# New values of a gated delta rule from (beta v - beta k state), the output norm's column sums one head later, and the last output tile in two token passes

## The chip, the cores and the metric

The kernel runs on one NeuronCore of a Trainium2 chip. The metric is the device time of the whole program in microseconds (us). Before the change it is 1100.43 us, the median of 3 runs (1100.04 to 1100.97).

## The reference

One decoder layer over 16 learned meta tokens and 512 tokens of width 1024, in float32. Two mixers work side by side (a gated delta rule of 8 heads, and a short gated convolution), are merged by gates and projected; a SwiGLU feed-forward block of width 2816 follows, and a last RMS norm. Cut to what matters here:

```python
# per head, chunks of 64 tokens
a_mat = jnp.where(strict, (k_beta @ k.T) * decay, 0.0)
rhs = jnp.concatenate([v_beta, k_beta * jnp.exp(gc)[..., None]], axis=-1)
sol = lax.linalg.triangular_solve(a_mat + eye, rhs, left_side=True, lower=True)
u_val, w_cum = sol[..., :dv], sol[..., dv:]
def step(state, xs):
    v_new = u_i - w_i @ state
    o_i = q_i @ state + qk_i @ v_new
    state = state * gl_i[..., None, None] + k_i.T @ v_new
    return state, o_i
o = rms_norm(o, o_norm) * jax.nn.silu(z)
...
h = h + mixed @ w_o
gt, up = jnp.split(rms_norm(h, norm2) @ w_gate_up, 2, axis=-1)
return h + (jax.nn.silu(gt) * up) @ w_down      # then the final rms_norm
```

With T = (a_mat + I)^-1 the new values are T (beta v) - (T (beta exp(gc) k)) state. They are also T (beta v - beta exp(gc) k state): the same sum, the solve last.

## The kernel before, in words

Everything lies transposed, features on the partitions and the 512 tokens (528 with the meta tokens) along the row. All weights come as one stream of 162 blocks of 128x1024 (`BLOCKS`, then `DOWN` blocks of the last projection). SyncE loads a block, ScalarE rounds it to its high part (`split_weights`, `w_hi`), GpSimd subtracts to get the low part (`w_lo`), and TensorE multiplies each of the block's 8 tiles three times (high by high, high by low, low by high; `products`, L911). So TensorE's stream is one long row of such products, 24 of 512 columns for a narrow block, 48 of 258 or 264 for a wide one.

The delta rule is woven into that stream. Each engine has a generator `delta_steps` with 28 steps a head; TensorE takes a step after every second tile, four a block, and the other engines take four in the period of a block, with the work on the last block's result (`evacuate`) and the splits of the next block's weights in between. Every engine runs its queue in order, the order is fixed by this code, and semaphores carry the rest. Seven blocks, and so one round of 28 steps, belong to a head: q, k, v, z, c, u, b. The rule's steps 0 to 3 lie in block b, 4 to 7 in the next head's q, and so on to 24 to 27 in its u.

A head's round, as the prediction uses it:

- Step 0, TensorE: K K^T (four 128x128 products, L972), turns of the meta tokens (L976, L977), turns of K (L981). VectorE: `am` (the masked matrix), then two operations on `tm`, three small ones, the short convolution's work on block u, and in step 1 `um`, the transpose of `tm` (L721), which the solve needs. Step 1, TensorE: Q K^T (L988).
- Step 3, TensorE: the solve's first product, `um` by `alev` (L1009); then it alternates to step 14 with ScalarE's copies and VectorE's updates.
- Step 15: W = K_beta T (four products, L1055), which ScalarE turns to `nwt`. Steps 16 to 22: for each of four pieces of 128 tokens the new values (`um` by `vb` and `nwt` by `state` in one bank, L1065 and L1066), ScalarE's copy `vnew`; steps 17 to 23: the state's update and the output.
- Steps 24 to 27: the output's norm. ScalarE squares the output (L505), VectorE adds the term of q (L765), ScalarE rounds (`qo_hi`), VectorE subtracts (`o_lo`), TensorE sums over the features with a matrix of ones (`spread_sums`, step 26), ScalarE takes the inverse root (L531), VectorE scales, ScalarE and GpSimd split the result (`og_hi`, `og_lo`). In the same steps the next head's k is normalised (k_root), its decay factors made (`decay_factors`, `xt`), its v turned (L1098) and scaled (`vb`).

At the end the last of 8 output tiles (L1160) has 66 products of 512 columns; then the tile is added to the residual (L902), squared (L644), summed by TensorE (L1166), the root taken (L646), all 8 tiles scaled (L905) and each sent out (L269).

Of the kernel before, what the change touches and what calls it, by code (L numbers as in the profile page):

```python
# [3 lines left out]
D = 1024  # L4
T = 512
META = 16
L = META + T
HALF = L // 2
TAIL = META - 4
HEADS = 8  # L10
# [15 lines left out]
DOWN = FT * KT // 8  # L26
STREAM = MAIN + DOWN
# [4 lines left out]
STEPS = 28  # L32
PRE = 20
# [28 lines left out]
def hybrid_block_kernel(nc, h_t, w_stream, w_ba, small, consts, out):  # L62
# [5 lines left out]
    with ctx:  # L68
        def sem(name):
            return ctx.enter_context(nc.semaphore(name))  # L70
        def sb(name, shape, dt=f32, where=ctx):
# [39 lines left out]
        kbe = sb("kbe", tile4, f32, mix_mem)  # L111
# [3 lines left out]
        nwt = sb("nwt", tile4, f32, mix_mem)  # L115
        osq = nwt
        pbx = nwt
# [43 lines left out]
        sb("um_split", tile4, f32, split_mem)  # L161
        qo_hi = sb("qo_hi", tile4, f32r, split_mem)
        sb("kdec_split", tile4, f32, split_mem)
# [51 lines left out]
        w_done, nwt_ready, vn_done, vn_ready, ds_done, state_ready, o_done = (  # L215
            sem(n) for n in ("w_done", "nwt_ready", "vn_done", "vn_ready", "ds_done", "state_ready", "o_done"))
# [7 lines left out]
            sem(n) for n in ("h2_squared", "sqf_ready", "last_sums", "y_ready"))  # L224
        def cols(ap, b, which):
            return ap.rearrange("p (g two b) -> p g two b", two=2, b=b)[:, :, which, :]
# [25 lines left out]
        def _(sp):  # L252
# [14 lines left out]
            for m in range(KT):  # L267
                sp.wait_ge(y_ready, m + 1)
                sp.dma_start(out[:, m, :], h1[:, m, :]).then_inc(stored, 16)  # L269
            sp.wait_ge(stored, 16 * KT)  # L270
        @block.gpsimd
        def _(pool):
# [14 lines left out]
            def split_weights(n, half):  # L287
                at = slice(512 * half, 512 * half + 512)
                pool.wait_ge(whi_ready, 2 * n + half + 1)
                if n >= 2:  # L290
                    pool.wait_ge(block_done, n - 1)
                nc.gpsimd.tensor_tensor(w_lo[:, n % 2, at], w_raw[:, n % 3, at], w_hi[:, n % 2, at].bitcast(f32),  # L292
                                        ALU.subtract).then_inc(wlo_ready, 1)
# [10 lines left out]
            def delta_steps():  # L304
                for h in range(-1, HEADS):
                    for step in range(0 if h >= 0 else PRE, STEPS):
# [21 lines left out]
                        if step == 27 and h >= 0:  # L328
                            pool.wait_ge(oghi_ready, h + 1)
                            nc.gpsimd.tensor_tensor(og_lo[:, h, :], flat(xd), og_hi[:, h, :].bitcast(f32),  # L330
                                                    ALU.subtract).then_inc(oglo_ready, 1)
# [16 lines left out]
            for n in range(STREAM + 1):  # L348
# [13 lines left out]
                else:  # L362
                    pool.wait_ge(sqf_ready, m)
                    nc.gpsimd.tensor_tensor(sqa[:, :], sqa[:, :], sqt[:, m % 2, :], ALU.add).then_inc(sqf_ready, 1)
        @block.scalar
        def _(act):
# [18 lines left out]
            def split_weights(n, half):  # L385
                at = slice(512 * half, 512 * half + 512)
                act.wait_ge(w_in[n % 3], 16 * (n // 3 + 1))
                if n >= 2:
                    act.wait_ge(block_done, n - 1)
                copy(w_hi[:, n % 2, at], w_raw[:, n % 3, at]).then_inc(whi_ready, 1)  # L390
# [60 lines left out]
            def delta_steps():  # L451
                for h in range(-1, HEADS):
                    nxt = h + 1
                    for step in range(0 if h >= 0 else PRE, STEPS):
# [5 lines left out]
                        if step == 1:  # L460
                            act.wait_ge(k_turned, h + 1)
                            for to, factor, first in ((kbe, be, 0), (kdec, erev, 1)):
                                for j in range(NJ):
                                    ins = nc.scalar.activation(to[:, j, :], dbank[0][:, 128 * j:128 * (j + 1)], ACT.Copy,
                                                               scale=factor[:, first + j, h:h + 1])
# [25 lines left out]
                        if step == 15:  # L491
                            act.wait_ge(w_done, h + 1)
                            nc.scalar.activation(flat(nwt), dbank[0][:, :], ACT.Copy, scale=-1.0).then_inc(nwt_ready, 1)
                        if step == 21 and nxt < HEADS:
                            act.wait_ge(km_sums, nxt + 1)
                            copy(sqm[:, :], dbank[1][:, 256:256 + META]).then_inc(km_copied, 1)
                        if 16 <= step <= 22 and step % 2 == 0 and h >= 0:
                            act.wait_ge(vn_done, NJ * h + (step - 16) // 2 + 1)
                            copy(vnew[:, :], dbank[1][:, 0:128]).then_inc(vn_ready, 1)
# [3 lines left out]
                        if step == 24 and h >= 0:  # L503
                            act.wait_ge(o_done, h + 1)
                            nc.scalar.activation(flat(osq), dbank[3][:, :], ACT.Square).then_inc(o_squared, 1)  # L505
                        if nxt < HEADS:
# [12 lines left out]
                            if step == 24 and h >= 0:  # L519
                                act.wait_ge(o_added, h + 1)  # L520
                                copy(flat(qo_hi), flat(osq)).then_inc(o_high, 1)
# [3 lines left out]
                        elif step == 24:  # L525
                            act.wait_ge(o_added, h + 1)
                            copy(flat(qo_hi), flat(osq)).then_inc(o_high, 1)
                        if h >= 0:
                            if step == 27:
                                act.wait_ge(o_sums, h + 1)  # L530
                                inverse_root(flat(osq), dbank[2][:, :], 1.0, 1).then_inc(o_root, 1)  # L531
                                act.wait_ge(ogf_ready, h + 1)
# [677 lines left out]
```

## Time and profile before

| | |
|---|---|
| median of 3 runs | 1100.43 us |
| the profiled execution, its own time | 1099.78 us |
| its span, first to last instruction | 1097.8 us |
| TensorE (PE) busy in the span | 1077.6 us, 98% |
| GpSimd (POOL), ScalarE (ACT), VectorE (DVE) busy | 551.3, 467.8, 339.0 us |
| TensorE in the chain that ended last | 95% |
| one head's round in that chain | 57.53 us |

The profile gives a row for each group of instructions: start, duration, engine, line, what is written and read. TensorE's durations are modelled and overlap: where rows follow each other without a wait, the distance between two starts is what an instruction costs. A float32 product of 128x128 shows two records. A bracket at a row's end is the engine's idle time ahead of it and what ended it.

### The profile page before, as it was taken

Reading aid. Unit: us, or ns where it says so; the run is one execution under the profiler, and the core shown is the slowest. Engines: PE = TensorE matmul, PEld = TensorE weight load, DVE = VectorE, ACT = ScalarE, POOL = GpSimd, SP = SyncE. Lnnn points to the kernel's source line nnn. Section 1 sums busy time; section 2 is a strip of 40 time slices with the busy share of each in tenths; the row PEclk is TensorE's granted clock in tenths of the full one; section 3 lists DMA queues with packets and bytes.
Section 4 is the critical chain, followed back from the end, with each engine's and each line's share of the span. In section 5 each row is a group of like instructions: output and inputs, shape, how many; then the busy total and the mean of one; then the engine's idle time right before and its main releaser. Section 6 shows DMA issues by size and latency. Waiting matters only on the chain.

```text
span 1097.8 us, 20326 instructions
## 1 busy us (share of the span) xinstructions
PE 1077.6 (98%) x8301; PEld 915.6 (83%) x8301; DVE 339.0 (31%) x595; ACT 467.8 (43%) x1027; POOL 551.3 (50%) x479
## 2 busy tenths in 40 slices
PE   6999999999999999999999999999999999999996
PEld 6999999999999898978788888878888888888884
DVE  6344545454554545351100112222111111200002
ACT  5565656564746564743422233443222233322221
POOL 4363545444453545363544555655555555555551
PEclk9999999999999999999999999999999999999998
DMA  4222212222212122122522322222232223232322
GB/s 180 75 83 69 78 59 70 78 68 76 72 60 87 60 68 79 59 66 71 173 95 80 112 78 96 96 96 96 96 96 87 92 91 96 97 96 96 96 77 77
DMA packets 27788, 95.45 MB, mean 87 GB/s; under 512 B 2984, under 2 KB 3240, under 8 KB 27696
## 3 DMA queue, kind: packets, MB, share of 16 engines
q1 hardware_dynamic: 26496, 91.77, 25.3%
q10 hardware_dynamic: 1200, 2.38, 0.6%
q8 instruction: 66, 1.08, 0.4%
q14 instruction: 26, 0.21, 0.1%
HBM read 92.03 MB, written 2.11 MB: 86 GB/s over the span
## 4 chain that ended last, share of the span: by engine, by line
PE 95%; DVE 2%; issue 1%; POOL 1%; ACT 0%; DMA 0%; DVEq 0%; SPq 0%; POOLq 0%
PE bank L910 94%; DVE qkv L668 0%; DVE h L905 0%; PE bank L981 0%; POOL w_lo L292 0%; DMA h_in<-h_t 0%; DVE qkv L660 0%; DVE cv L668 0%; PE bank L1098 0%; DVE x_lo L672 0%; POOL x_lo L298 0%; PE bank L977 0%; PE bank L976 0%; ACT cbuf L397 0%; DVE h L902 0%
## 5 line engine op out<-in xcount | busy, mean ns | idle before, releaser
L292 POOL TENSOR_TENSOR w_lo<-w_raw,w_hi 128x512 fp32r<-128x512 f32 x324 | 426.1, 1333 | 489.4 <-ACT w_hi L373 489.3
L910 PE MATMUL bank<-x_hi,w_hi 128*128 128x258 f32 (+2 forms) x896 | 248.2, 335 | 5.5 <-DVE x_lo L672 4.5
L373 ACT ACTIVATE w_hi<-w_raw 128x512 fp32r<-128x512 f32 x324 | 190.1, 623 | 107.1 <-PE bank L910 106.7
L910 PE MATMUL bank<-x_hi,w_lo 128*128 128x258 f32 (+2 forms) x896 | 230.6, 316 | 0.0
L910 PE MATMUL bank<-x_lo,w_hi 128*128 128x258 f32 (+2 forms) x896 | 230.1, 315 | 0.0
L910 PE MATMUL bank<-og_hi,w_hi 128*128 128x512 f32 x416 | 164.7, 396 | 0.0
L910 PEld LDWEIGHTS bank<-x_hi,w_hi 128*128 128x128 f32 x896 | 147.0, 189 | 21.0 <-issue 4.3
L910 PE MATMUL bank<-og_hi,w_lo 128*128 128x512 f32 x416 | 164.3, 395 | 0.0
L910 PE MATMUL bank<-og_lo,w_hi 128*128 128x512 f32 x416 | 164.3, 395 | 0.0
L910 PEld LDWEIGHTS bank<-x_hi,w_lo 128*128 128x128 f32 x896 | 147.0, 188 | 11.2
L910 PEld LDWEIGHTS bank<-x_lo,w_hi 128*128 128x128 f32 x896 | 147.5, 189 | 8.6
L910 PEld LDWEIGHTS bank<-og_lo,w_hi 128*128 128x128 f32 x416 | 78.0, 187 | 19.4 <-issue 0.2
L910 PEld LDWEIGHTS bank<-og_hi,w_lo 128*128 128x128 f32 x416 | 78.0, 187 | 19.2
L910 PEld LDWEIGHTS bank<-og_hi,w_hi 128*128 128x128 f32 x416 | 78.0, 187 | 19.1 <-issue 0.2
L800 DVE SCALAR_TENSOR_TENSOR cv<-raw,sm,cv 128x528 f32<-128x528 f32 (+1 forms) x72 | 62.4, 867 | 40.8 <-ACT raw L373 39.9
L910 PE MATMUL bank<-f_hi,w_hi 128*128 128x512 f32 x176 | 69.9, 397 | 0.0
L910 PE MATMUL bank<-f_lo,w_hi 128*128 128x512 f32 x176 | 69.5, 395 | 0.0
L910 PE MATMUL bank<-f_hi,w_lo 128*128 128x512 f32 x176 | 69.5, 395 | 0.0
L910 PE MATMUL bank<-yb_hi,w_hi 128*128 128x512 f32 x128 | 51.5, 402 | 0.8 <-POOL w_lo L292 0.8
L910 PE MATMUL bank<-yb_hi,w_lo 128*128 128x512 f32 x128 | 50.6, 395 | 0.0
L910 PE MATMUL bank<-yb_lo,w_hi 128*128 128x512 f32 x128 | 50.6, 395 | 0.0
L373 ACT ACTIVATE f_hi<-ff 128x512 fp32r<-128x512 f32 x22 | 13.9, 633 | 84.3 <-DVE ff L655 84.3
(240 smaller groups left out, 1276.6 us busy)
## 6 DMA issues: line engine op xcount, KB each, us to landing
w_raw<-w_stream SPq DMA_DIRECT2D x162, 512.0 KB, 3.3
h_in<-h_t SPq DMA_DIRECT2D x4, 528.0 KB, 5.0
h<-h_t ACTq DMA_DIRECT2D x1, 2048.0 KB, 9.8
out<-h SPq DMA_DIRECT2D x8, 256.0 KB, 2.1
h_in<-gc_dram SPq DMA_DIRECT2D x7, 264.0 KB, 3.2
cst<-consts SPq DMA_DIRECT2D x1, 512.0 KB, 8.0
h_in<-gc_dram ACTq DMA_DIRECT2D x1, 264.0 KB, 3.0
sm<-small SPq DMA_DIRECT2D x1, 80.5 KB, 6.1
```

What stands on the lines that cost most here:

```text
L292: nc.gpsimd.tensor_tensor(w_lo[:, n % 2, at], w_raw[:, n % 3, at], w_hi[:, n % 2, at].bitcast(f32), ALU.subtract).then_inc(wlo_ready, 1)
L373: return nc.scalar.activation(to, x, ACT.Copy)
L800: ins = nc.vector.scalar_tensor_tensor(to, xj, taps[:, j:j + 1], to, ALU.mult, ALU.add)
L910: return nc.tensor.matmul(o, w, x, start=start, stop=stop)
```

## The change

Delta rule. W, its copy `nwt` and the scaled copy `kbe` are gone. The normalised K is kept in a tile of its own (`kn`). In each piece TensorE now multiplies K by the state first; VectorE makes beta v minus the scaled product in place (`vb`, with `be` now negative), and TensorE applies the solve to that. A piece's steps are three, not two: 14, 17, 20, 23 (K by state), 15, 18, 21, 24 (solve), 16, 19, 22, 25 (state and output). Q K^T moves from step 1 to 5, the turns of K from 0 to 7, `kdec` to 8; the meta sums of k from step 21 to 22.

Output norm. The square moves from step 24 to 26, the add to 26, `qo_hi` and `o_lo` to 27, the column sums and the root to step 1 of the next head, the scaling to 3, `og_hi` to 4, `og_lo` to 5. After head 8's last step a rest of six steps (`TRAIL`) holds these. The second load of h is issued two blocks later.

Last tile. It is computed for tokens 0 to 255 and then 256 to 511, with 256-column products, over the same three weight blocks; the last block's split parts lie in `og_hi` and `og_lo`. The first half's norm and output run beside the second half. Tiles 0 to 6 are multiplied by the norm's weights ahead of time, and each half is then scaled in three operations of VectorE and one of GpSimd.

```diff
-                        if step == 1:
+                        if step == 8:
                             act.wait_ge(k_turned, h + 1)
...
-                        if 16 <= step <= 22 and step % 2 == 0 and h >= 0:
-                            act.wait_ge(vn_done, NJ * h + (step - 16) // 2 + 1)
+                        if 15 <= step <= 24 and step % 3 == 0 and h >= 0:
+                            act.wait_ge(vn_done, NJ * h + (step - 15) // 3 + 1)
...
-                        if step == 24 and h >= 0:
+                        if step == 26 and h >= 0:
                             act.wait_ge(o_done, h + 1)
                             nc.scalar.activation(flat(osq), dbank[3][:, :], ACT.Square).then_inc(o_squared, 1)
+                        if step == 27 and h >= 0:
+                            act.wait_ge(o_added, h + 1)
+                            copy(flat(qo_hi), flat(osq)).then_inc(o_high, 1)
...
+                        if step == 1 and h >= 1:
+                            act.wait_ge(o_sums, h)
+                            inverse_root(flat(osq), dbank[0][:, :], 1.0, 1).then_inc(o_root, 1)
...
+                        if 14 <= step <= 23 and step % 3 == 2 and h >= 0:
+                            j = (step - 14) // 3
+                            dve.wait_ge(vb_ready, h + 1)
+                            dve.wait_ge(ks_done, NJ * h + j + 1)
+                            nc.vector.scalar_tensor_tensor(vb[:, j, :], dbank[0][:, 128 * j:128 * (j + 1)], be[:, j, h:h + 1],
+                                                           vb[:, j, :], ALU.mult, ALU.add).then_inc(r_ready, 1)
...
-                        if step == 15:
-                            pe.wait_ge(u_updated, len(LEVELS) * (h + 1))
-                            for j in range(NJ):
-                                ins = mm(dbank[0][:, c128[j]], kbe[:, j, :], um[:, j, :])
-                            ins.then_inc(w_done, 1)
...
-                            mm(dbank[1][:, 0:128], um[:, j, :], vb[:, j, :], stop=False)
-                            mm(dbank[1][:, 0:128], nwt[:, j, :], state[:, :], start=False).then_inc(vn_done, 1)
+                            mm(dbank[0][:, c128[j]], kn[:, j, :], state[:, :]).then_inc(ks_done, 1)
...
+                            mm(dbank[1][:, 0:128], um[:, j, :], vb[:, j, :]).then_inc(vn_done, 1)
...
+            for half in range(2):
+                for k in range(FT):
...
+                    ins = products([big[(KT - 1) % 2][half][:, 0:T // 2]], MAIN + d, i, [f_hi[:, k, th[half]]],
+                                   [f_lo[:, k, th[half]]], k == 0, k == FT - 1)
...
+                    if half == 1 and k == 5:
+                        pe.wait_ge(half_squared, 1)
+                        mm(dbank[0][:, 0:T // 2], ones, sqt[:, (KT - 1) % 2, th[0]], start=False).then_inc(last_sums, 1)
+                ins.then_inc(half_done, 1)
```

Three places in the queues, first before the change and then after it. VectorE at the end of a head (steps 25 to 27) and in step 0 of the next; `nwt` is the tile of squares before (`osq` after), and the row `am<-bank,am` is step 0. Before:

```order
L655 TENSOR_TENSOR qkv<-qkv,am 128x512
L695 TENSOR_TENSOR o_lo<-nwt,qo_hi 128x512 [waits o_high]
L655 TENSOR_TENSOR am<-xt,beta 128x512 [waits k_ready,xd_ready]
L655 TENSOR_TENSOR xt<-xt,cst 128x512
L655 TENSOR_TENSOR vb<-bank,beta 128x512 [waits v_turned]
L790 SCALAR_TENSOR_TENSOR xd<-bank,on_scaled,nwt 128x512 [waits o_root]
L655 TENSOR_TENSOR xd<-xd,zs 128x512 [waits zs_ready,dve_chain]
L655 TENSOR_TENSOR am<-bank,am 128x512 [waits xb_ready,kk_done]
```

After, the same place:

```order
L686 TENSOR_TENSOR kn<-qkv,am 128x512
L686 TENSOR_TENSOR am<-xt,beta 128x512 [waits k_ready,xd_ready]
L686 TENSOR_TENSOR xt<-xt,cst 128x512
L686 TENSOR_TENSOR vb<-bank,beta 128x512 [waits v_turned]
L829 TENSOR_TENSOR osq<-osq,h_in 128x512 [waits q_squared,o_squared]
L727 TENSOR_TENSOR o_lo<-osq,qo_hi 128x512 [waits o_high]
L686 TENSOR_TENSOR am<-bank,am 128x512 [waits xb_ready,kk_done]
```

The add and `o_lo` now stand behind `vb`, and the two operations on `xd` have left the place. ScalarE at steps 24 to 27. Before:

```order
L505 ACTIVATE nwt<-bank 128x512 [waits o_done]
L375 ACTIVATE sqm<-sqm,eps 128x16 [waits km_copied,k_sums]
L376 ACTIVATE sqm<-sqm 128x16 [waits act_chain]
L375 ACTIVATE am<-bank,eps 128x512
L376 ACTIVATE am<-am 128x512 [waits act_chain]
L373 ACTIVATE qo_hi<-nwt 128x512 [waits o_added]
L373 ACTIVATE cbuf<-bank 128x258 [waits yblo_ready,block_done]
```

After:

```order
L399 ACTIVATE vnew<-bank 128x128 [waits vn_done]
L401 ACTIVATE sqm<-sqm,eps 128x16 [waits km_copied,k_sums]
L402 ACTIVATE sqm<-sqm 128x16 [waits act_chain]
L401 ACTIVATE am<-bank,eps 128x512
L402 ACTIVATE am<-am 128x512 [waits act_chain]
L399 ACTIVATE cbuf<-bank 128x258 [waits yblo_ready,block_done]
```

The square and `qo_hi` have left, and the copy of the last piece's new values (`vnew`), which waits for TensorE's step 24, now stands ahead of the roots of k. ScalarE at the last head's norm, when the gates' blocks run; `w_hi` is a weight split. Before:

```order
L373 ACTIVATE w_hi<-w_raw 128x512 [waits block_done,w_in2] x2
L375 ACT_TABLE_LOAD
L375 ACTIVATE nwt<-bank,eps 128x512 [waits o_sums]
L376 ACT_TABLE_LOAD
L376 ACTIVATE nwt<-nwt 128x512 [waits act_chain]
L373 ACTIVATE og_hi<-xd 128x512 [waits ogf_ready]
L373 ACTIVATE w_hi<-w_raw 128x512 [waits block_done,w_in0] x2
```

After:

```order
L399 ACTIVATE qo_hi<-osq 128x512 [waits o_added]
L401 ACT_TABLE_LOAD [waits o_sums]
L401 ACTIVATE osq<-bank,eps 128x512 [waits block_done]
L402 ACT_TABLE_LOAD
L402 ACTIVATE osq<-osq 128x512 [waits act_chain]
L399 ACTIVATE w_hi<-w_raw 128x512 [waits block_done,w_in0] x2
L399 ACTIVATE og_hi<-xd 128x512 [waits ogf_ready]
```

The wait for the column sums stands on the table load itself now, ahead of it; `og_hi` has moved behind the weight splits.

## Rows read from the trace of the kernel before

**Rows 1.** The page, busy time by engine: us, share of the span, instructions.
```profile
PE 1077.6 (98%) x8301; PEld 915.6 (83%) x8301; DVE 339.0 (31%) x595; ACT 467.8 (43%) x1027; POOL 551.3 (50%) x479
```
**Rows 2.** Timeline of PE: start us, us, engine, line, op, out<-in. Step 15.
```profile
155.98 1.05 PE L910 MATMUL bank<-um,kbe 128*128 128x128 f32 x8
...
157.10 0.40 PE L910 MATMUL bank<-x_lo,w_hi 128*128 128x512 f32 x1
```
**Rows 3.** Timeline of PE, from a head's step 24 to the next one's step 3.
```profile
117.06 0.60 PE L1098 MATMUL bank<-cst,qkv 128*128 128x128 f32 x4
...
123.69 1.05 PE L910 MATMUL bank<-qkv 128*128 128x128 f32 x8
...
125.04 0.66 PE L981 MATMUL bank<-cst,qkv 128*128 128x128 f32 x4
125.45 0.48 PE L910 MATMUL bank<-x_hi,w_hi 128*128 128x512 f32 x1
...
130.70 0.44 PE L910 MATMUL bank<-um,alev 32*32 32x16 f32 x32
```
**Rows 4.** Timeline of ACT over the same head's end.
```profile
113.46 0.28 ACT L373 ACTIVATE vnew<-bank 128x128 f32<-128x128 f32 x1
...
116.07 0.30 ACT L375 ACTIVATE sqm<-sqm,eps 128x16 f32<-128x16 f32 x1
...
117.76 0.62 ACT L373 ACTIVATE qo_hi<-nwt 128x512 fp32r<-128x512 f32 x1
...
119.76 0.62 ACT L449 ACTIVATE xt<-xt 128x512 f32<-128x512 f32 x1
```
**Rows 5.** Timeline of DVE over the same stretch.
```profile
121.90 0.68 DVE L655 TENSOR_TENSOR vb<-bank,beta 128x512 f32<-128x512 f32 x1
...
124.78 0.69 DVE L655 TENSOR_TENSOR am<-bank,am 128x512 f32<-128x512 f32 x1 [0.61 <-PE bank L910]
...
129.61 0.71 DVE L721 STREAM_TRANSPOSE um<-tm 128x512 f32<-128x512 f32 x1
```
**Rows 6.** Timeline of DVE in the last head: the add and o_lo, qo_hi between.
```profile
517.65 0.69 DVE L765 TENSOR_TENSOR nwt<-nwt,h_in 128x512 f32<-128x512 f32 x1 [4.20 <-ACT nwt L505]
...
519.12 0.69 DVE L695 TENSOR_TENSOR o_lo<-nwt,qo_hi 128x512 fp32r<-128x512 f32 x1 [0.77 <-ACT qo_hi L373]
```
**Rows 7.** Timelines of DVE and PE in the first head: its transpose, its step 3.
```profile
71.53 0.71 DVE L721 STREAM_TRANSPOSE um<-tm 128x512 f32<-128x512 f32 x1
...
73.17 0.44 PE L910 MATMUL bank<-um,alev 32*32 32x16 f32 x32
```
**Rows 8.** Timelines of ACT and PE at the last head's norm.
```profile
520.56 1.28 ACT L375 ACT_TABLE_LOAD   x1
521.86 0.69 ACT L375 ACTIVATE nwt<-bank,eps 128x512 f32<-128x512 f32 x1
...
521.01 0.40 PE L910 MATMUL bank<-qo_hi,ones_r 128*128 128x512 f32 x1
...
529.42 0.47 PE L910 MATMUL bank<-yb_hi,w_hi 128*128 128x512 f32 x1 [0.78 <-POOL w_lo L292]
```
**Rows 9.** Timeline of PE: two of the wide block's pairs, eight pairs apart.
```profile
118.22 0.41 PE L910 MATMUL bank<-x_hi,w_hi 128*128 128x258 f32 x2
...
120.14 0.40 PE L910 MATMUL bank<-x_hi,w_lo 128*128 128x258 f32 x2
```
**Rows 10.** Timeline of POOL: splits of the last block but one.
```profile
1068.91 2.55 POOL L292 TENSOR_TENSOR w_lo<-w_raw,w_hi 128x512 fp32r<-128x512 f32 x2 [3.06 <-ACT w_hi L373]
```
**Rows 11.** Timeline of all engines at the end.
```profile
1085.37 0.39 PE L910 MATMUL bank<-f_hi,w_lo 128*128 128x512 f32 x1
...
1087.20 1.12 PE L910 MATMUL bank<-sqt,ones_mem 128*128 128x512 f32 x2 [1.45 <-ACT sqt L644]
...
1089.75 5.39 DVE L905 SCALAR_TENSOR_TENSOR h<-h,sm,rs 128x512 f32<-128x512 f32 x8 [3.26 <-ACT rs L376]
```
**Rows 12.** Windows: stretch, us, busy us of PE, PEld, DVE, ACT, POOL, PE clock, DMA share, GB/s.
```profile
1093.00:1094.00 1.00, 0.00 (x0) 0.00 (x0) 1.00 (x3) 0.00 (x0) 0.00 (x0) 0.50 1.01 385
```

More of the change, by code:

```diff
@@ L26 @@
 DOWN = FT * KT // 8
+LAST_FIRST = FT * (KT - 1)
+LAST_SCALED = [slice(0, 3), slice(3, 5)]
+LAST_POOL = slice(5, 7)
 STREAM = MAIN + DOWN
@@ L266, in _ @@
                 sp.dma_start(w_raw[:, n % 3, :], w_stream[n, :, :]).then_inc(w_in[n % 3], 16)
[L267 to L270, printed above, removed]
+            for i, half in enumerate(th):
+                for j, group in enumerate(LAST_SCALED):
+                    sp.wait_ge(y_ready, 3 * i + j + 1)
+                    sp.dma_start(out[:, group, half], h1[:, group, half]).then_inc(stored, 16)
+                sp.wait_ge(yp_ready, i + 1)
+                sp.dma_start(out[:, LAST_POOL, half], h1[:, LAST_POOL, half]).then_inc(stored, 16)
+                sp.wait_ge(y_ready, 3 * i + 3)
+                sp.dma_start(out[:, KT - 1:KT, half], h1[:, KT - 1:KT, half]).then_inc(stored, 16)
+            sp.wait_ge(stored, 16 * 8)
         @block.gpsimd
@@ L304, in delta_steps @@
             def delta_steps():
-                for h in range(-1, HEADS):
-                    for step in range(0 if h >= 0 else PRE, STEPS):
+                for h in range(-1, HEADS + 1):
+                    for step in range(0 if h >= 0 else PRE, STEPS if h < HEADS else TRAIL):
+                        if step == 5 and h >= 1:
+                            pool.wait_ge(oghi_ready, h)
+                            nc.gpsimd.tensor_tensor(og_lo[:, h - 1, :], flat(xd), og_hi[:, h - 1, :].bitcast(f32),
+                                                    ALU.subtract).then_inc(oglo_ready, 1)
+                        if h == HEADS:
+                            yield
+                            continue
                         if step == 0:
@@ L964, in delta_steps @@
                 qh, kh, vh = qkv[:, 0, :], qkv[:, 1, :], qkv[:, 2, :]
-                for h in range(-1, HEADS):
+                for h in range(-1, HEADS + 1):
                     nxt = h + 1
-                    for step in range(0 if h >= 0 else PRE, STEPS):
+                    for step in range(0 if h >= 0 else PRE, STEPS if h < HEADS else TRAIL):
+                        if h == HEADS:
+                            if step == 1:
+                                pe.wait_ge(o_split, h)
+                                spread_sums(dbank[0], flat(qo_hi), flat(o_lo)).then_inc(o_sums, 1)
+                            yield
+                            continue
                         if step == 0:
@@ L1089, in delta_steps @@
                                 spread_sums(dbank[2], flat(k_hi), flat(k_lo)).then_inc(k_sums, 1)
-                        if step == 26 and h >= 0:
-                            pe.wait_ge(o_split, h + 1)
-                            if nxt < HEADS:
-                                pe.wait_ge(k_root, nxt + 1)
-                            spread_sums(dbank[2], flat(qo_hi), flat(o_lo)).then_inc(o_sums, 1)
                         if step == 24 and nxt < HEADS:
```

249 lines of the change are left out of this document (145 added, 104 removed).

## The prediction

> **What bounds it.** I read the page's busy times first: PE is at work for 1077.6 of 1097.8 us [rows 1]. Then the timeline of PE: in the heads its products follow each other at fixed distances, with no bracket of idle time. So each instruction taken off PE is worth its distance to the next, as long as nothing that PE waits for becomes late. Then the timelines of ACT and DVE beside it, to see how early each thing is that PE will want. Outside the heads I look at two places: the last head's norm, where PE does wait, 0.78 us for a weight split [rows 8], and the end, where PE has finished and 12.4 us remain (last product at 1085.37 [rows 11], span 1097.8).
>
> **Removed from PE.** W is four float32 products in each of 8 heads. They start at 155.98, and the second weight product behind them at 157.10 [rows 2]; without them it would start one distance of 0.23 (the usual 512-column product's) after 155.98. So W costs 157.10 - 155.98 - 0.23 = 0.89 us, 0.22 a product. The other products keep their number: K by state stands for `nwt` by state. Other groups of two and three such products scale in the same way, so cutting a piece into three groups costs nothing that I can see; bound it by 1 us in all, either way. Removed: 8 x 0.89 = **-7.1 us**. The copies `nwt` and `kbe` lie on ACT, which is not the bound.
>
> **A head's turn, heads 1 to 7.** This is what decides. PE comes to step 3 (`um` by `alev`, which waits for the transpose `um`) earlier, and DVE makes `um` later.
>
> PE. From step 0 at 123.69 to step 3 at 130.70 [rows 3]. Gone from between: the turns of K, 125.45 - 125.04 = 0.41, and Q K^T, four float32 products like W, 0.89. New: the column sums, two 512-column products, 0.47. Step 3 would start at 130.70 - 0.41 - 0.89 + 0.47 = 129.87, if step 0 stays at 123.69.
>
> DVE. Even undelayed `um` ends at 129.61 + 0.71 = 130.32 [rows 5]: 0.45 late, with the 0.04 us of a release 0.5. And it is delayed. Count back from step 0: the turns of v are at 117.06, 6.63 before it [rows 3]; in that stretch the sums go (-0.47) and one product of 0.22 comes between, so they start at 117.30 and the last piece's solve product at 117.08. Its result is there 0.38 + 0.04 later, 117.50. ACT copies `vnew`: 0.28 in its row, 0.10 of it under the next [rows 4], so the roots of k begin at 117.68 (116.07 before). From there to the exponential of `xt` were 119.76 - 116.07 = 3.69 us, with `qo_hi` in it, 0.62 less the 0.10 of overlap; now 3.17: `xt` at 120.85, 1.09 later than before. DVE's three operations behind it keep their distance, so `vb` starts at 121.90 + 1.09 = 122.99 [rows 5]. Here the order rows show the add and `o_lo` pushed in. `vb` takes 0.60 to the next; the square is done by 123.0, so the add does not wait; from add to `o_lo` across ACT's `qo_hi` are 519.12 - 517.65 = 1.47 [rows 6]; and 0.60 more to `am`. So `am` starts at 122.99 + 0.60 + 1.47 + 0.60 = 125.66 and not 124.78 [rows 5]: 0.88 late. All up to `um` follows in order, so it ends at 131.20, and PE waits 131.24 - 129.87 = 1.37 us. The chain starts at PE's own step 24, so it repeats in each head. GpSimd's split of block q ends near 130.9 by the same delay and hides under this wait. 7 x 1.37 = **+9.6 us**; bounds 0.5 (no delay of DVE) and 1.7 (0.3 more, from DVE operations that slow down beside GpSimd), 3.5 to 11.9 in all.
>
> **Head 0** has no norm before it. `um` ends at 72.24 + 0.04; PE's step 3 moves from 73.17 [rows 7] by 0.41 + 0.89 to 71.87. **+0.4 us.**
>
> **The last head's norm.** The sums now lie at step 1, in the middle of a block; from their start s the next block is due at s + 0.47 + 12 x 0.233 = s + 3.27. ACT stands in order: before, the table load at 520.56 was issued ahead of the sums (521.01), and the logarithm followed at 521.86 [rows 8]. Now the load waits for the sums, and both roots stand ahead of the next block's splits. s + 0.68 load, 1.30 to the logarithm, 0.69, load 1.28, exponential 0.63 and two gaps of 0.02: s + 4.6; split on ACT 0.53 more, 0.15 of gaps, GpSimd 1.28 (half of the row in [rows 10]), and PE starts at s + 6.6. It waits 3.35 us, where before it waited 0.78 idle and 0.16 under the tail of the product before, 0.94 [rows 8]. **+2.4 us**; if the load is hidden after all, +1.1.
>
> Rows 8 show the load followed by its logarithm 1.30 us from its start. The Trainium skill, ScalarE: Activation LUTs, section "What ACT_TABLE_LOAD costs", puts a switch at 2.66 us, a drain of 1.38 on top of the load. By that page the two loads would put 2.8 us more on this wait, 1105.5 in all; the trace does not agree, as nothing lies between 520.56 and 521.86 but the load.
>
> **The end.** The 132 products of 256 columns: eight pairs of 258 columns take 120.14 - 118.22 = 1.92 us, 0.12 each [rows 9], against 0.233 for 512: 15.84 - 15.4 = +0.45. The first half's sums stand inside, half of 1.12 [rows 11]: PE's last product comes 1.0 us later. Behind it, before: 12.43 us. Now, on 256 columns, add, square, sums, logarithm, exponential take about 2.9 instead of 4.38 (1085.37 to 1089.75 [rows 11]). Then three DVE operations, about 2.0 instead of 5.39; the first transfer starts at about 3.8, its bytes 0.8 later. A half is 1.05 MB; at 385 GB/s [rows 12] 2.7 us, and 0.6 to the end: 8.0. Rows of 1 KB are not in the trace; at half the rate it is 10.7. Gain 12.4 - 8.0 - 1.0 = 3.4, at the bad end 0.7; I take **-3.0 us**, as the nearest row has 2 KB rows at full rate.
>
> The Trainium skill, DMA: Bandwidth & Descriptors, section "Specifications", asks for 512 B at least; by it the 1 KB rows go at full rate and the gain is 3.4. No run here shows it yet.
>
> **Sum.** -7.1 + 9.6 + 0.4 + 2.4 - 3.0 = +2.3 us. The profiled execution took 1099.78 us (span 1097.8 and 2 around it), 0.65 under the median; it would be 1102.1, the median 1100.43 + 2.3 = 1102.7. The vnew, state and K-by-state links lie a step apart (1.4 us and more) with work of 0.3 to 0.7 us, so I cost their new waits at nothing. If one were short it would be the same on 28 or 32 places.
>
> **Rivals.**
> 1. The turn costs only what PE's early arrival costs. For it: DVE has 0.61 idle before `am` [rows 5] and chains through three engines can be shorter than I add up. Against: the queue order is fixed. Place: `am` in step 0; it decides if `am` starts at 124.8 still. Price 0.5 a head: -7.1 + 3.5 + 0.4 + 2.4 - 3.0 = -3.8, **1096.6, faster**. Chance 0.20.
> 2. As forecast, but the last norm's load does not hold ACT up: 1101.4. Against: the wait stands on the load. Chance 0.15.
> 3. As forecast, with transfers of 1 KB rows at half rate: +2.7 - 0.4, **1105.0**. Chance 0.13.
> 4. The two passes use up weights in half the time: a block of 8 tiles lasts 2.9 us in the first pass, GpSimd needs 2.55 a block [rows 10]. GpSimd starts the last block but one at 1068.91, when the block two ahead of it is done; the first pass starts 1.4 us after that block's end of 1068.0, at 1069.4, and has 6 tiles (2.2 us) until it wants the first half at 1071.6 (ready 1070.2), the second at 1073.0 (ready 1071.46): 1.5 us of cover. The last block and the squares' sum stand behind and have about as much. If the cover goes, 1 to 2 us: 1104.2. Chance 0.07.
> 5. A gain I do not see, such as fewer changes between product kinds on PE: 2 to 4 us over the eight heads; 1099. Chance 0.05.
>
> **Chances.** Forecast 0.40, by its terms 1100.8 to 1104.2. A difference under 0.2% (2.2 us) can hardly be told from none: faster is below 1098.2, slower above 1102.6. The forecast gives 0.25 to slower and 0.15 to same; rival 1 faster 0.19 and same 0.01; rival 2 same 0.13, slower 0.02; 3 slower 0.13; 4 slower 0.05, same 0.02; 5 same 0.03, faster 0.02. Faster 0.21, same 0.34, slower 0.45. The range leaves out the ends of 1 and 3: 1096.8 to 1105.8.
>
> **What would show it.** Right: a bracket of 1.2 to 1.6 us on `um` by `alev` in heads 1 to 7, put down to DVE's `um`, 0.4 in head 0; a round of about 58.0 us against 57.53; one wait of about 3 us on a weight split near the last norm; PE's end about 1 us later against the sum of the rest, and 8 to 9 us behind it. Wrong: no bracket there (rival 1 or less), waits on `vb`, `vnew` or `state` in steps 14 to 25, or on `w_lo` in the last tile.

## The result, and the profile after

The changed kernel takes **1107.74 us**, the median of 4 runs (1105.83 to 1108.52), against 1100.43 before: ratio 1.0069, 95% interval 1.0056 to 1.0081. It is slower by 0.7%. The forecast was 1102.7 with a range up to 1105.8: the direction was right, the size was not. The profiled execution is the fastest of the four, 1105.83 us against 1099.78 of the one profiled before: +6.05 us.

The page's busy times, to lay beside [rows 1]:

```profile
PE 1075.6 (97%) x8307; PEld 916.0 (83%) x8307; DVE 353.0 (32%) x626; ACT 460.6 (42%) x999; POOL 553.6 (50%) x481
```

TensorE's busy time fell by 2.0 us while the span grew by 6.2 (1097.8 to 1104.0). So TensorE stands idle more often, and the view to read is its list of waits. Columns: what PE ran, what it waited for, us in total, times, the longest.

```profile
PE bank L959 <- DVE um L762: 8.0, 8, 1.1
PE bank L959 <- DVE x_lo L703: 3.6, 4, 2.5
PE bank L959 <- POOL w_lo L310: 3.2, 1, 3.2
PE bank L959 <- ACT mu L399: 2.7, 7, 0.5
```

The wait for `x_lo` lies ahead of the heads, and stood in the kernel before with 4.5 us. The other three lines carry the result. `um` (8.0 us in 8 heads) and the one wait for `w_lo` (3.2) were forecast. `mu`, in the last line, is ScalarE's copy of a 16x16 matrix; it comes in seven heads, and the prediction has no term for it. The timeline of TensorE shows the waits for `um` and for `mu` in one head, 4.5 us apart:

```profile
187.24 0.40 PE L959 MATMUL bank<-x_hi,w_lo 128*128 128x512 f32 x1
188.72 0.44 PE L959 MATMUL bank<-um,alev 32*32 32x16 f32 x32 [1.09 <-DVE um L762]
...
192.45 0.41 PE L959 MATMUL bank<-x_hi,w_lo 128*128 128x258 f32 x2
193.21 1.02 PE L959 MATMUL bank<-qkv,kn 128*128 128x128 f32 x7 [0.34 <-ACT mu L399]
```

Read the distances, not the brackets alone. From 187.24 to 188.72 are 1.48 us where 0.23 would do (0.32 in the kernel before). The bracket says 1.09, since the modelled end of the product before it (the product and its tail) covers the rest.

Ahead of `um` stand the add and `o_lo`, where the prediction put them. VectorE and GpSimd there:

```profile
181.20 1.17 DVE L829 TENSOR_TENSOR osq<-osq,h_in 128x512 f32<-128x512 f32 x1
183.06 0.69 DVE L727 TENSOR_TENSOR o_lo<-osq,qo_hi 128x512 fp32r<-128x512 f32 x1 [0.69 <-ACT qo_hi L399]
```
```profile
180.21 1.61 POOL L310 TENSOR_TENSOR w_lo<-w_raw,w_hi 128x512 fp32r<-128x512 f32 x1 [0.68 <-ACT w_hi L399]
```

The add takes 1.17 us, where it took 0.69 before. So `am` starts at 183.67, 2.32 behind step 0 (181.35), against 1.09 before: 1.23 late. The operation on `tm` behind it takes 0.43 where it took 0.97, and `um` ends 7.31 behind step 0, against 6.63 before: 0.68 late.

TensorE is led to `mu` by VectorE and ScalarE. Their timelines in the same stretch, with GpSimd's:

```profile
187.95 0.71 DVE L762 STREAM_TRANSPOSE um<-tm 128x512 f32<-128x512 f32 x1
188.59 0.71 DVE L870 SCALAR_TENSOR_TENSOR cv<-raw,sm,cv 128x512 f32<-128x512 f32 x1
189.33 1.33 DVE L874 SCALAR_TENSOR_TENSOR cv<-raw,sm,cv 128x512 f32<-128x512 f32 x1
190.58 0.74 DVE L737 SCALAR_TENSOR_TENSOR xd<-bank,on_scaled,osq 128x512 f32<-128x512 f32 x1
191.36 0.98 DVE L686 TENSOR_TENSOR xd<-xd,zs 128x512 f32<-128x512 f32 x1
```
```profile
192.37 0.63 ACT L399 ACTIVATE og_hi<-xd 128x512 fp32r<-128x512 f32 x1 [2.73 <-DVE xd L686]
192.91 0.16 ACT L399 ACTIVATE mu<-bank 16x16 f32<-16x16 f32 x1
```
```profile
189.38 0.73 POOL L297 TENSOR_TENSOR alev<-am,cst 128x256 f32<-128x256 f32 x1 [1.07 <-DVE cv L870]
190.06 1.73 POOL L310 TENSOR_TENSOR w_lo<-w_raw,w_hi 128x512 fp32r<-128x512 f32 x1
```

`mu` waits for nothing of its own: its input was made just behind 190.77, by a 16x16 product. It stands behind `og_hi` in ScalarE's queue, and `og_hi` waits 2.73 us for the gated output `xd`, which VectorE makes in two operations behind the short convolution's. That is the moved norm: `og_hi` used to stand in step 27 and now stands in step 4 ahead of `mu`.

The last head's norm, which the forecast put at 3.35 us, in ScalarE's and TensorE's timelines (answering to [rows 8]):

```profile
532.76 1.28 ACT L401 ACT_TABLE_LOAD   x1 [3.86 <-PE bank L959]
534.06 0.69 ACT L401 ACTIVATE osq<-bank,eps 128x512 f32<-128x512 f32 x1
534.76 1.28 ACT L402 ACT_TABLE_LOAD   x1
536.06 0.63 ACT L402 ACTIVATE osq<-osq 128x512 f32<-128x512 f32 x1
```
```profile
532.05 0.40 PE L959 MATMUL bank<-qo_hi,ones_r 128*128 128x512 f32 x1
...
538.69 0.47 PE L959 MATMUL bank<-yb_hi,w_hi 128*128 128x512 f32 x1 [3.21 <-POOL w_lo L310]
```

From the sums to the block behind them are 538.69 - 532.05 = 6.64 us; the forecast said 6.6.

The end, against [rows 11]:

```profile
1095.28 0.28 PE L959 MATMUL bank<-f_hi,og_lo 128*128 128x256 f32 x1
...
1096.52 0.70 PE L959 MATMUL bank<-sqt,ones_mem 128*128 128x256 f32 x2 [0.96 <-ACT sqt L673]
...
1098.18 1.55 DVE L950 TENSOR_TENSOR h<-h,bank 128x768 f32<-128x768 f32 x2 [2.17 <-ACT bank L676]
```

Behind TensorE's last product of weights lie 1104.0 - 1095.28 = 8.72 us, before 12.43.

**The sum as measured**, in the profiled execution. A head's round (start of the column sums to the next head's) is 58.57 us against 57.53, +1.04 in seven heads. The step-3 group costs 1.72 us against 0.56 (+1.16 a head, +8.1 in all), the group behind `mu` 2.09, where Q K^T (0.89) and the small products of that step (0.60) alone would take 1.49 (+0.60 a head, +4.2), W is gone (-0.89). Head 0's step 3: +0.4. Last norm: +2.4. Last tile: 16.72 us instead of 16.02, +0.7, and 3.7 less behind it. Together -7.1 + 8.1 + 4.2 + 0.4 + 2.4 + 0.7 - 3.7 = +5.0; 1.05 us of the 6.05 stay without a row. They lie in the rounds, where the terms (-0.89 + 1.16 + 0.60 = 0.87) fall short of 1.04 by 0.17 a head. The trace shows where in a round: the distances from one weight product of the wide blocks to the next add up to 28.47 us, against 28.30 before, in equal number. One more of them than before (18, not 17) is the first behind a group of other products, 0.22 us instead of 0.12, which is some 0.1; what makes the rest is open.

### The profile page after: what moved, and what is told of

The parts are those of the page before. It is cut to its first block, busy times and chain, and to the rows that moved or that the text cites. A ratio compares the mean times of both kernels' runs of the same rounds, so it can differ in the third digit from the quotient of the medians.

```text
span 1104.0 us, 20381 instructions
## 1 busy us (share of the span) xinstructions
PE 1075.6 (97%) x8307; PEld 916.0 (83%) x8307; DVE 353.0 (32%) x626; ACT 460.6 (42%) x999; POOL 553.6 (50%) x481
## 4 chain that ended last, share of the span: by engine, by line
PE 85%; DVE 7%; issue 4%; ACT 3%; POOL 0%; DVEq 0%; ACTq 0%; POOLq 0%
PE bank L959 85%; DVE osq L829 1%; DVE xd L686 1%; DVE cv L862 1%; DVE am L686 1%; DVE um L762 1%; DVE raw L686 0%; DVE xd L737 0%; DVE qkv L699 0%; DVE xt L686 0%; DVE cv L870 0%; ACT qo_hi L399 0%; ACT og_hi L399 0%; ACT cbuf L399 0%; DVE vb L686 0%
## 5 line engine op out<-in xcount | busy, mean ns | idle before, releaser
L310 POOL TENSOR_TENSOR w_lo<-w_raw,w_hi 128x512 fp32r<-128x512 f32 x322 | 420.0, 1322 | 493.4 <-ACT w_hi L399 493.4
L959 PE MATMUL bank<-f_hi,w_hi 128*128 128x512 f32 (+1 forms) x182 | 68.8, 378 | 0.0
L959 PE MATMUL bank<-f_lo,w_hi 128*128 128x512 f32 (+1 forms) x182 | 68.7, 377 | 0.0
L959 PE MATMUL bank<-f_hi,w_lo 128*128 128x512 f32 (+1 forms) x182 | 68.6, 377 | 0.0
L686 DVE TENSOR_TENSOR tg<-bank,rs 128x512 f32<-128x512 f32 x22 | 15.2, 692 | 110.2 <-PE bank L959 101.7
```

The costliest lines, as they stand in the source:

```text
L310: nc.gpsimd.tensor_tensor(low_weights(n)[:, at], w_raw[:, n % 3, at], high_weights(n)[:, at].bitcast(f32), ALU.subtract).then_inc(wlo_read ...
L686: return nc.vector.tensor_tensor(to, a, b, ALU.mult)
L959: return nc.tensor.matmul(o, w, x, start=start, stop=stop)
```

## The experiments

Ten runs. Medians; the kernel before, run beside them on the same chip each time, had 1100.10 to 1100.17.

**1. The last tile alone.** The kernel before with only the change of the last output tile:

```diff
-            for m in range(KT):
-                sp.wait_ge(y_ready, m + 1)
-                sp.dma_start(out[:, m, :], h1[:, m, :]).then_inc(stored, 16)
+            for i, half in enumerate(th):
+                for j, group in enumerate(LAST_SCALED):
+                    sp.wait_ge(y_ready, 3 * i + j + 1)
+                    sp.dma_start(out[:, group, half], h1[:, group, half]).then_inc(stored, 16)
...
```

> The kernel before with only the last tile in two token passes (and its early scaling and output). By my sum, read again from the trace after: TensorE's last product 0.7 us later, the end behind it 3.7 us shorter, so 3.0 us faster than before: about 1097.4 us. Rival: the tail's gain is smaller than its rows show, since the weights of the last two blocks or the 1 KB output rows come late when TensorE is not already delayed: within 1 us of before.

Measured: 1096.92 us (1096.44 to 1097.18), ratio 0.9969 (0.9958 to 0.9981): -3.25. The tail's term holds, and this part beats the kernel before.

**2. All but the last tile.** The changed kernel with that part undone; the rule and the norm stay:

```diff
-            for i, half in enumerate(th):
...
+            for m in range(KT):
+                sp.wait_ge(y_ready, m + 1)
+                sp.dma_start(out[:, m, :], h1[:, m, :]).then_inc(stored, 16)
```

> The changed kernel with the last output tile put back as it was (512-column products, one norm, eight scalings, eight transfers); the delta rule and the output norm stay changed. If the parts add, it is the change without the tail's 3.25 us: 1105.83 + 3.3 = about 1109.1 us in an execution without a lowered clock at the last norm, 1110.5 to 1112 us in one with it, and 1110 to 1111 us as a median. Rival (the tail's gain depends on the state in which PE reaches it): more than 1.5 us off.

Measured: 1110.75 us (1110.35 to 1112.07), ratio 1.0100 (1.0086 to 1.0114). Against the change this is +3.0 (+2.8 against the repeat of it in run 6): the two parts add, and the delta rule with its norm costs 10.65 us by itself.

**3. What W was worth.** The kernel before, with one product of W's four; it leaves out the other three, so its output is not the reference's.

```diff
-                            for j in range(NJ):
-                                ins = mm(dbank[0][:, c128[j]], kbe[:, j, :], um[:, j, :])
-                            ins.then_inc(w_done, 1)
+                            mm(dbank[0][:, c128[0]], kbe[:, 0, :], um[:, 0, :]).then_inc(w_done, 1)
```

> The kernel before with one of the four products of the group W instead of four, so its numbers aren't the reference's; everything else stands. It prices the work that the change took off TensorE. The recorded forecast took W's four products as 0.89 us a head, all of it on the path: three of four gone, the four-product row's 0.22 us a product gives 3 x 0.22 x 8 = -5.3 us, 1095.1 us. Rival: TensorE only comes early to its next wait (the forecast's first rival, a gain of little or nothing inside a head): 1098.5 to 1100.2 us.

Measured: 1094.46 us (1094.43 to 1095.45), -5.7; the profiled one -5.26. A head's round is 56.87 us instead of 57.53: 0.66 for three products, 0.22 each. What leaves TensorE in the middle of a head is time gained in full. The -7.1 is right, and the reason for the loss has to be sought in what came in its place.

**4. One table load ahead of the last norm's wait.**

```diff
                         if step == 1 and h >= 1:
+                            if h == HEADS:
+                                nc.scalar.preload_act_table_set("natural_log_exp_and_others")
                             act.wait_ge(o_sums, h)
```

> The changed kernel with one table load, for logarithm and exponential together, issued ahead of the wait for the last head's column sums. Two loads of 1.28 us leave the chain from the sums to the next weight split. Theory: TensorE's wait there falls from 3.2 us idle to 0.6 to 0.7, the profiled time from 1105.8 to 1103.3. Second theory, on the medians: the runs of the changed kernel with a mean clock of 0.994 owe it to this wait; then here all runs show 0.997 and the median falls by 4 us or more, to about 1103.5. Rival: the clock has nothing to do with it; the median falls by 2.5 us and some runs still show 0.994.

Measured: 1103.78 us (1103.32 to 1103.96), ratio 1.0031 (1.0019 to 1.0044). TensorE's wait there shrank:

```profile
PE bank L961 <- POOL w_lo L310: 0.8, 2, 0.6
```

Profiled against profiled the gain is 2.0 us, but median against median 4.0, and the spread went from 2.7 us to 0.6. So the long wait seems to cost more than it lasts in most executions; runs 5 and 6 follow that. The second theory had the time right and its sign wrong: the six executions show mean clocks of 0.994 to 0.996, and none shows 0.997. An execution's mean clock doesn't tell what happens at this wait, since it holds other lowered stretches too (the last section names one).

**5. The same delay in the kernel before.**

```diff
                             if step == 27:
                                 act.wait_ge(o_sums, h + 1)
+                                if h == HEADS - 1:
+                                    for s in ("sigmoid_and_others", "exp_and_others", "natural_log_exp_and_others"):
+                                        nc.scalar.preload_act_table_set(s)
```

> The kernel before, with two more table loads on ScalarE behind its wait for the last head's output sums. It lays nothing but a delay of 2 x 1.28 = 2.6 us at the place where the change's last norm waited 3.2 us for the split of the weights. Theory 1 (the delay costs what it lasts, once): 1100.4 + 2.3 to 2.6 = about 1102.8 us. Theory 2 (a TensorE idle for some 3 us there also gets a lower granted clock behind it, in some or all executions): 1104 to 1105.5 us in the executions where the mean clock is 0.994, and 1102.8 us in those where it is 0.997.

Measured: 1103.57 us (1102.21 to 1104.19), ratio 1.0029 (1.0018 to 1.0041). The edit has three loads, where the expectation says two more: they stand in place of the one ahead of the logarithm, and the one between logarithm and exponential falls away, so the exponential starts 2.58 us later (526.44 against 523.86).

```profile
521.85 3.86 ACT L533 ACT_TABLE_LOAD   x3 [1.14 <-PE bank L913]
```

The profiled execution took 1103.56. Its timeline of PE, and its windows (stretch, us, busy us of PE, granted clock, DMA share, GB/s):

```profile
528.43 0.40 PE L913 MATMUL bank<-x_hi,w_lo 128*128 128x512 f32 x1
531.95 0.50 PE L913 MATMUL bank<-yb_hi,w_hi 128*128 128x512 f32 x1 [3.13 <-POOL w_lo L292]
532.26 0.62 PE L913 MATMUL bank<-yb_lo,w_hi 128*128 128x512 f32 x1
532.68 0.63 PE L913 MATMUL bank<-yb_hi,w_lo 128*128 128x512 f32 x1
```
```profile
532.00:533.00 1.00, 1.00 (x3) 0.63 0.00 0
533.00:534.00 1.00, 1.00 (x4) 0.50 0.00 0
534.00:535.00 1.00, 1.00 (x4) 0.50 0.79 254
```

TensorE stood idle for 3.1 us, began again, and then ran at half its full clock (1.2 instead of 2.4 GHz) until 535.7: products 0.43 us apart, not 0.23. Eight products at 0.19 more are 1.5 us on top of the wait. The first theory (the delay costs what it lasts, 1102.8) misses by 0.8. The second has the half clock right, but not its times: it wanted 1104 us or more wherever the mean clock is 0.994, and the executions at 0.993 to 0.994 took 1102.86 to 1104.19.

**6. The change once more.**

> The changed kernel itself, once more, to see whether its executions that take 1107 to 1108.5 us are those in which TensorE's granted clock falls behind the 3.2 us wait at the last head's norm, as it did in the kernel before with that wait put in. Theory: a profiled execution over 1107 us has a granted clock of 0.5 for some 3 us behind that wait, and products 0.43 us apart there instead of 0.23; one near 1105.8 us has not. Rival: the slower executions show a full clock there, and lose their 2 us elsewhere.

Measured: 1107.94 us (1107.22 to 1108.53), ratio 1.0072 (1.0058 to 1.0086); this time the profiled execution is one of the slower ones, 1108.04. The same two views:

```profile
539.35 0.47 PE L959 MATMUL bank<-yb_hi,w_hi 128*128 128x512 f32 x1 [3.21 <-POOL w_lo L310]
...
539.89 0.61 PE L959 MATMUL bank<-yb_hi,w_lo 128*128 128x512 f32 x1
```
```profile
538.00:539.00 1.00, 0.00 (x0) 1.00 0.00 0
539.00:540.00 1.00, 0.65 (x3) 0.95 0.00 0
540.00:541.00 1.00, 1.00 (x4) 0.50 0.00 0
...
542.00:543.00 1.00, 1.00 (x4) 0.50 0.83 287
```

In the execution of 1105.83 us the same wait was followed by a full clock:

```profile
539.00:540.00 1.00, 1.00 (x6) 1.00 0.00 0
540.00:541.00 1.00, 1.00 (x6) 1.00 0.00 0
```

The theory of run 6 stands: of the 2.2 us between these two executions 1.5 come behind the wait, with the half clock. That the other executions near the median hold it too is likely, not shown; none of them was profiled. The remaining 0.66 us had come before the wait (539.35 against 538.69), in the first head. There ScalarE waited for a transfer of the decay rows that the faster execution had in time, and the weight split behind it came late:

```profile
59.52 1.28 ACT L467 ACTIVATE xt<-h_in,ngc 128x128 f32<-128x128 f32 x4 [1.03 <-DMA h_in<-gc_dram]
```
```profile
65.26 0.47 PE L959 MATMUL bank<-x_hi,w_hi 128*128 128x512 f32 x1 [0.61 <-POOL w_lo L310]
```

Neither bracket is in the profile of 1105.83 us. So single profiled executions differ by up to 0.7 us from this place alone.

**7. `mu` ahead of `og_hi`.**

```diff
                         if step == 4 and h >= 1:
                             act.wait_ge(ogf_ready, h)
                             copy(og_hi[:, h - 1, :], flat(xd)).then_inc(oghi_ready, 1)
...
-                        if step == 4:
-                            act.wait_ge(mt_turned, h + 1)
-                            copy(mu[:, :], dbank[0][0:META, 0:META]).then_inc(mu_ready, 1)
```

The three lines taken away stand, for heads 0 to 7, ahead of the first three.

> The changed kernel with ScalarE's 16x16 copy mu ahead of og_hi in step 4, so that it no longer waits behind the scaled output. Theory: the 0.34 us of idle time on TensorE at step 5 of heads 1 to 7 (0.62 us each with what the group costs more) goes, 7 x 0.62 = 4.3 us faster than the changed kernel, and nothing else moves. Rival: VectorE is late as well (its update of um comes behind the scaling of the output), so TensorE waits for um instead and under 1 us comes back.

Measured: 1103.1 us (1101.98 to 1103.83), ratio 1.0027 (1.0017 to 1.0037): 4.6 less than the change. The wait for `mu` is gone from the list, the one for `um` unchanged (8.0 in 8), the round 57.97 us: 0.60 less, the size read from the rows. The cause is shown. Profiled against profiled the gain is only 2.4, since this execution (1103.42) has the half clock behind the last norm that the change's fastest had not; up to that norm it had gained the 4.2.

**8. The transpose `um` right behind `tm`,** ahead of VectorE's `ma` and the short convolution.

```diff
+                            dve.wait_ge(t_ready, h + 1)
+                            nc.vector.transpose(flat(um), flat(tm)).then_inc(u_ready, 1)
                             dve.wait_ge(mpre_done, h + 1)
                             dve.wait_ge(mx_ready, h + 1)
                             nc.vector.scalar_tensor_tensor(ma[:, :], mbank[0:META, 256:272], beta[0:META, 0, h:h + 1], mx[:, :],
...
```

> The changed kernel with VectorE's transpose um right behind tm in step 0, ahead of the three small operations and the short convolution's work (0.7 + 0.8 + 0.8 us). Theory: um is ready about 2.2 us earlier, before TensorE's step 3, and the 1.1 us bracket goes in heads 1 to 7 and 0.4 in head 0: up to 8.5 us faster than the changed kernel, less what the wait for mu at step 5 then takes back, as the scaling of the output is not earlier: TensorE is at step 5 1.1 us sooner, so the wait there grows from 0.6 to about 1.7 us and the net gain is near zero to 2 us. Rival: the two waits are independent, and 8 us come back.

Measured: 1110.15 us (1109.56 to 1111.81), ratio 1.0093 (1.0079 to 1.0107): slower than the change by 2.4. The theory and its rival both missed. The list of waits says why:

```profile
PE bank L958 <- POOL w_lo L310: 12.4, 10, 3.2
PE bank L958 <- ACT mu L399: 4.3, 7, 0.7
```

The wait for `um` is gone, and 9.2 us (12.4 less the last norm's 3.2) are now waited for the low half of the next weights. `ma` comes one transpose later; GpSimd's `mt` needs `ma`, and GpSimd's split stands behind `mt`:

```profile
187.67 0.21 POOL L297 TENSOR_TENSOR mt<-ma,cst 16x16 f32<-16x16 f32 x1 [1.21 <-DVE ma L757]
...
188.68 1.26 POOL L310 TENSOR_TENSOR w_lo<-w_raw,w_hi 128x512 fp32r<-128x512 f32 x1
```

Here lies what the prediction meant by "hides under this wait". In the change the split ended at 188.30, only 0.36 us ahead of `um` (188.66), so it was a second cause at the same place; counted from the sums, it now ends 0.75 later (4.84 against 4.09).

**9. The roots of k ahead of the last piece's `vnew`,** on ScalarE in step 24.

```diff
+                        if nxt < HEADS and step == 24:
+                            act.wait_ge(k_sums, nxt + 1)
+                            act.wait_ge(km_copied, nxt + 1)
+                            inverse_root(sqm[:, :], sqm[:, :], 1.0, 0)
+                            inverse_root(flat(am), dbank[2][:, :], 1.0, 0).then_inc(k_root, 1)
                         if 15 <= step <= 24 and step % 3 == 0 and h >= 0:
...
```

> The changed kernel with ScalarE's four root instructions of the next head's k ahead of its copy of the last piece's new values in step 24, as they stood in the kernel before (there the copy was in step 22). ScalarE waited 2.11 us for that product with the roots and the rest of the norm's and the decay's work queued behind it. Theory (this queued wait makes the output norm late, the norm holds VectorE at o_lo for 0.69 us, and the block transpose um and the copy mu are late by it): um comes 0.7 us earlier in seven heads, mu 0.3, together 1105.8 - 7 x (0.7 to 1.0) = 1099 to 1101 us profiled. Rival (VectorE's own work between the mask and um sets um, whatever comes before): within 1 us of 1105.8 profiled, and the wait for um stays at 8.0 us in 8.

Measured: 1104.33 us (1103.33 to 1105.15), ratio 1.0037 (1.0024 to 1.0049); 3.4 less than the change, profiled 2.5 less with a lowered clock (0.83 in the ten us from 530) that the change's fastest execution had not. VectorE's `am`, 0.54 us before the sums in the change (183.67 against 184.21), comes 1.76 before them (181.81 against 183.57). The list:

```profile
PE bank L959 <- POOL w_lo L310: 5.4, 8, 3.2
PE bank L959 <- ACT mu L399: 4.4, 7, 0.7
```

The wait for `um` is gone from heads 1 to 7 (0.4 is left in head 0): the stretch from ScalarE's queued `vnew` to `um`, which the prediction built, was the cause of it. But 0.3 us a head are left for `w_lo`, and `mu` waits longer, since TensorE now comes to it sooner. The round is 58.00 instead of 58.57: of the 1.16 us, 0.57 came back, and about 0.32 went to `w_lo` and 0.24 to `mu`. For that reason, and by the half clock, the profiled 1103.33 lies above the expected 1099 to 1101.

**10. Three orders at once:** 4, 7 and 9.

> The changed kernel with three orders of ScalarE altered at once: a table loaded ahead of the wait for the last sums, the copy mu ahead of the high half of the gated output, and the roots of k ahead of the last piece's new values. If the three causes are separate, their gains add: 1105.8 - 2.4 - 4.3 - 5 = about 1094 us. If the wait at mu and the wait at um are one lateness seen twice, the sum is less: 1097 to 1099 us.

Measured: **1093.83 us** (1093.46 to 1094.10), ratio to the kernel before 0.9943 (0.9929 to 0.9956). It beats both kernels: 6.3 us under the one before, 13.9 under the change. What is left on the list of waits in the heads:

```profile
PE bank L961 <- POOL w_lo L310: 3.1, 9, 0.6
PE bank L961 <- DVE um L764: 0.3, 1, 0.3
```

A round takes 57.15 us: 1.42 less than the change's, more than 0.57 and 0.60 together. Beside 9 alone it is 0.85 less, since `mu` had grown by what `um` gave back. Against the kernel before a head gains 0.38 of the 0.89 that W is worth; 0.3 is the rest of `w_lo`, 0.2 is open (about the 0.17 that the change's rounds leave). Some 3 of the 6.3 us are the last tile's (run 1); the delta rule and norm in these orders were not run without it.

## Why the prediction was right and wrong, by its steps

- **Removed from PE, -7.1: right.** Run 3 prices a product at 0.22 us on the path.
- **A head's turn, `um`, +9.6: right in kind, a little large.** 1.16 a head, not 1.37; 8.1, and a bracket of 1.09 where 1.2 to 1.6 was the sign of being right. Run 9 shows the cause, the norm's work on ScalarE and VectorE behind a queued `vnew`. The working took VectorE's delay as 0.88 us and carried it through to `um` unchanged. It was 1.23 at `am`, since the add took 1.17 us, and 0.68 at `um`, since the operation on `tm` took 0.54 less than before: two errors that partly cancel.
- **The end of a head's turn, put at nothing: the step that failed.** The working follows TensorE to step 3 and stops there; new waits of the heads were looked for in steps 14 to 25 only ("so I cost their new waits at nothing"). The move of `og_hi` from step 27 to 4 puts a wait for VectorE ahead of `mu` in an in-order queue, and the prediction never named what is queued behind it. The round was forecast at about 58.0 us and is 58.57. The wait costs 0.60 us in seven heads, 4.2; run 7 gives it back.
- **Head 0, +0.4: right. Last norm, +2.4: right in one execution.** TensorE's wait is what was worked out, 3.37 us with its tail against 3.35. That a wait of that length leaves a half clock behind it in most executions has no term; it costs 1.5 us where it was profiled (runs 5 to 7), and the median of the change fits one with it. Nothing in the trace of before shows so long a wait at that place.
- ScalarE's rows at the last norm have 534.06 - 532.76 = 1.30 us from a load to the logarithm, as in [rows 8]. The Trainium skill, ScalarE: Activation LUTs, section "What ACT_TABLE_LOAD costs", counts a drain of 1.38 beside the load; this trace does not agree, as nothing but the load fits between the two starts.
- **The end, -3.0: right.** The last tile costs 0.7 more, not 1.0; behind it 3.7 less, not 4.4; together -3.0, where the prediction took 3.0 out of its 3.4. Run 1 has -3.25 in all.
- **Steps 14 to 25 at nothing: right.** No wait there is in the list.
- **A piece in three groups, "nothing that I can see", bounded by 1 us: right within its bound.** The one more first product behind a group is some 0.1 us a head, as said above.
- The rest: 1.05 us in the profiled execution without a term, of which that 0.1 a head is a part.

From the forecast to the median: 1102.7 - 1.5 (`um`) + 4.2 (`mu`) + 1.05 (without a term) + 1.5 (half clock) = 1107.95, against 1107.74.

The range ended at 1105.8, just behind rival 3's 1105.0. It should have held a second wait in the heads, of half the size of the first: one operation moved in a queue costs at the same place seven times. Of the rivals, the first is answered by the bracket on `um` and by `am` starting late, the third by the output's rate (last section), the fourth by the list, which has no wait for `w_lo` in the last tile.

## What to carry to other kernels

A step that is moved brings its wait with it, so list what stands behind it on that in-order queue, however small: a 16x16 copy of 0.16 us held TensorE for 0.6 us in each of seven heads. Where an engine waits, look at the second latest thing too (here the weight split behind `um`), since clearing the first alone may gain nothing or lose. And a saving on the bound engine is kept only if the queues that feed it are put in the order of their new deadlines: the same change was 0.7% slower, and with three such orders 0.6% faster than before (half of that is the last tile's).

## What the runs showed of the hardware

- A TensorE idle for 3.1 to 3.2 us at full clock fell to half clock around the time it began again in six profiled executions (runs 2, 5, 6, 7, 8 and 9), for 3.4 us in five of them and 6.8 in run 2, and stayed at full clock in one with the same wait (the change at 1105.83 us). The fall is recorded between 0.7 us ahead of the first product (run 2) and 1.2 behind it (run 9). It makes 1.5 of the 2.2 us between two executions of one program.
- All twelve profiles, the kernel before among them, have an idle stretch of 2.5 us on TensorE that ends near 17 us. Behind it nine show half clock for 3.4 or 6.8 us, and three (before, runs 2 and 7) none. It costs little there, where TensorE also waits for other things: with 3.4 us of it the change and with 6.8 us of it the repeat of run 6 come to 25 us of the span within 0.15 us of each other.
- VectorE's operations with two inputs in SBUF take longer beside GpSimd's. The add on `osq` takes 1.17 us beside a split and 0.69 in the kernel before, where no GpSimd instruction overlaps it. The convolution's operation at L874 takes 1.33 us in the change and 0.84 in the kernel before (L835), at the same shape; it overlaps GpSimd's `alev` and `w_lo` in both, with other starts, and that split takes 1.73 us in both, where undisturbed ones take 1.27 to 1.30. The Trainium skill, SBUF — State Buffer, section "SBUF: two separate sides", says that VectorE and GpSimd share one pair of ports, which one of them holds for a whole instruction. The rows of the add agree with it: the split that began first ends at 181.82, and the add ends 0.55 us behind that. No run moved one of the two away from the other.
- The output's transfers with rows of 1 KB went at 340 and 344 GB/s in the change's two full microseconds at the end, those with rows of 2 KB at 371 to 387 in the kernel before [rows 12]: a tenth slower, not half. The transfers also differ in their number and in the tiles that each holds, so that the row's length is the cause is not shown. The window of the changed kernel:

```profile
1102.00:1103.00 1.00, 0.00 (x0) 0.00 (x0) 0.00 (x0) 0.00 (x0) 0.00 (x0) 0.50 0.96 344
```
